# RWKV token shift into a buffer of its own, mixed by GpSimd beside the selective attention

## What is computed

```python
for l in range(DEPTH):                                  # DEPTH = 2
    h = rms_norm_2(x, norm_mix[l])
    cols_a, cols_b, gate_a, gate_b = split_cols(h @ w_in[l], IN_SIZES)   # 1792, 1224, 1024, 1024 columns
    y_a, v_first = rwkv7_branch(cols_a, v_first, rwkv_mu[l], ...)
    y_b = dsa_branch(cols_b, ...)                       # selective attention: 64 keys of 256 for each query
    merged = (sigmoid(gate_a) * (y_a @ w_branch_a[l]) + sigmoid(gate_b) * (y_b @ w_branch_b[l]))
    x = x + merged @ w_out[l]
...
def rwkv7_branch(cols, v_first, mu, ...):
    cols = cols + (token_shift(cols) - cols) * mu       # token_shift: row t gets row t - 1, row 0 gets zeros
    r, k, v, wd, ad, gd = split_cols(cols, RWKV_SIZES)
    w_log = -softplus(-(w0 + tanh(wd) @ w2)) - 0.5
    a = sigmoid(a0 + ad @ a2)
    g = sigmoid(gd) @ g2
...
```

## Time and profile before

| | before |
|---|---|
| median of 3 runs | 3055.31 us |
| lowest and highest | 3055.24 and 3057.67 us |
| the profiled execution | 3050.5 us |
| its span, first to last instruction | 3048.7 us |
| TensorE (matmuls) busy | 2824.4 us, 93% |
| VectorE (DVE) busy | 1524.6 us, 50% |
| ScalarE (ACT) busy | 1037.8 us, 34% |
| GpSimd (POOL) busy | 124.1 us, 4% |
| mean granted TensorE clock | 0.972 |

### The profile page before, as it was taken

The page is one execution under the profiler, slowest core; times in us unless marked ns, Lnnn a source line. Parts: engine busy times, 40 slices in busy tenths (PEclk is TensorE's granted clock), DMA queues, the critical chain, the costliest instruction groups (busy, mean ns, idle before and its releaser), DMA issues.

```text
span 3048.7 us, 34473 instructions
## 1 busy us (share of the span) xinstructions
PE 2824.4 (93%) x14731; PEld 2086.1 (68%) x14731; DVE 1524.6 (50%) x1814; ACT 1037.8 (34%) x1240; POOL 124.1 (4%) x109
## 2 busy tenths in 40 slices
PE   8996999999999999998879999998799889999998
PEld 6774576887878576884437458855374578888887
DVE  3555515445554524443564345435653356666587
ACT  3432223343443223431220133413201245445465
POOL 0002000000011100000002000000020000000000
PEclk9998999999999999998999999999899899999999
DMA  6552144556544153554341435543404056566596
GB/s 251 208 166 83 56 153 151 175 195 200 185 163 155 56 186 121 204 166 138 102 129 33 151 116 202 183 154 98 133 30 154 19 207 227 201 217 228 198 317 240
DMA packets 226724, 484.01 MB, mean 159 GB/s; under 512 B 11694, under 2 KB 45102, under 8 KB 226126
## 3 DMA queue, kind: packets, MB, share of 16 engines
q1 hardware_dynamic: 226192, 478.16, 46.2%
q10 hardware_dynamic: 380, 3.66, 0.4%
HBM read 477.07 MB, written 2.95 MB: 157 GB/s over the span
## 4 chain that ended last, share of the span: by engine, by line
PE 80%; DVE 11%; DMA 3%; ACT 2%; issue 2%; SPq 1%; POOL 0%; ACTq 0%; DVEq 0%; POOLq 0%
PE psum L406 21%; PE psum L403 16%; PE psum L405 16%; PE psum L404 16%; PE psum L1932 2%; PE psum L761 2%; PE psum L524 1%; PE psum L736 1%; PE psum L2662 1%; DMA weight_ring<-in_ffn_w_gate 1%; PE psum L2018 1%; DVE weight_ring_low_halves L398 1%; DVE stage_area_halves L515 1%; ACT weight_high_halves L392 1%; PE psum L746 1%
## 5 line engine op out<-in xcount | busy, mean ns | idle before, releaser
L398 DVE TENSOR_TENSOR weight_ring_low_halves<-weight_ring,weight_high_halves 128x2048 fp32r<-128x2048 f32 (+2 forms) x306 | 656.1, 2156 | 638.0 <-ACT weight_high_halves L392 638.0
L403 PE MATMUL psum<-weight_high_halves,stage_area_halves 128*128 128x512 f32 (+2 forms) x2266 | 875.8, 386 | 56.5 <-DVE stage_area_halves L515 37.7
L405 PE MATMUL psum<-weight_high_halves,stage_area_halves 128*128 128x512 f32 (+2 forms) x2266 | 866.4, 382 | 0.0
L404 PE MATMUL psum<-weight_ring_low_halves,stage_area_halves 128*128 128x512 f32 (+3 forms) x2060 | 788.2, 383 | 0.0
L392 ACT ACTIVATE weight_high_halves<-weight_ring 128x2048 fp32r<-128x2048 f32 (+2 forms) x306 | 551.6, 1812 | 592.5 <-PE psum L405 338.2
L406 PE MATMUL psum<-weight_ring,stage_area 128*128 128x512 f32 (+2 forms) x1600 | 666.4, 577 | 9.2 <-issue 6.6
L406 PEld LDWEIGHTS psum<-weight_ring,stage_area 128*128 128x128 f32 x1600 | 301.5, 191 | 357.5 <-issue 352.4
L403 PEld LDWEIGHTS psum<-weight_high_halves,stage_area_halves 128*128 128x128 f32 x2266 | 431.2, 190 | 146.0 <-issue 25.5
L405 PEld LDWEIGHTS psum<-weight_high_halves,stage_area_halves 128*128 128x128 f32 x2266 | 430.7, 190 | 86.6
L404 PEld LDWEIGHTS psum<-weight_ring_low_halves,stage_area_halves 128*128 128x128 f32 x2060 | 392.0, 190 | 75.5
L505 ACT ACTIVATE stage_area<-psum 128x512 f32<-128x512 f32 (+3 forms) x138 | 76.4, 561 | 702.2 <-PE psum L406 359.9
(11 more groups left out here) (265 smaller groups left out, 2240.4 us busy)
## 6 DMA issues: line engine op xcount, KB each, us to landing
weight_ring<-in_ffn_w_down SPq DMA_DIRECT2D x44, 1024.0 KB, 5.0
weight_ring<-in_ffn_w_gate SPq DMA_DIRECT2D x40, 1024.0 KB, 5.2
weight_ring<-in_ffn_w_up SPq DMA_DIRECT2D x40, 1024.0 KB, 5.1
weight_ring<-in_w_in SPq DMA_DIRECT2D x36, 1024.0 KB, 5.1
weight_ring<-in_moe_wd SPq DMA_DIRECT2D x30, 1024.0 KB, 4.9
weight_ring<-in_moe_wg SPq DMA_DIRECT2D x23, 1024.0 KB, 6.6
weight_ring<-in_moe_wu SPq DMA_DIRECT2D x23, 1024.0 KB, 7.3
weight_ring<-in_mem_w_kv SPq DMA_DIRECT2D x16, 1024.0 KB, 5.1
```

The source lines that it names most:

```text
L398: v.raw.tensor_tensor(self.low_half(name), self.in_slot(name), self.high_half(name), ALU.subtract).then_inc(*v.mark("low_halves", ("halves ...
L403: pe.raw.matmul(out, a[1], w[0], start=start, stop=False)
L404: pe.raw.matmul(out, a[0], w[1], start=False, stop=False)
L405: return pe.raw.matmul(out, a[0], w[0], start=False, stop=stop)
```

## The change

- The shifted rows get a buffer of their own, `shifted_rows`, over the last two slots of `weight_high_halves`, which nothing uses in this stage. VectorE clears row 0 of it ahead of the selective attention's preparation, after a wait for the last four split pieces (L2412 of the new kernel).
- ScalarE issues the three DMAs of the shift right behind the copies of the `a_in` projection, in front of its copies of the turned queries and keys.
- `mix_vector` becomes `mix_gpsimd`: the same three operations, on GpSimd (L1721, L1724, L1726 of the new kernel). VectorE waits for `mixed` after the attention.
- `mu` is no longer a parameter load that waits for the end of the attention. It is a piece of the weight ring, between the pieces of gate block (0, 0) and (0, 1).
- The vectors `vec` wait for the end of the attention, not for `mixed`. Their place in SyncE's queue, behind the pieces of gate block (1, 1), is unchanged.

```diff
@@ Net.__init__
+            self.shifted_rows = names.enter_context(nc.sbuf_tensor("shifted_rows", [P, (HIGH_SLOTS - 2) * SLOT], F32))
+            names.enter_context(nc.sbuf_tensor("up_to_norm_params", [P, 2 * MT * D], F32))
@@ Second.__init__
-        self.colsS = net.part(E, MT, N_A)
-        self.mu = net.part(16896, N_A)
+        self.colsS = net.shifted_rows[:, 0:MT * N_A].rearrange("p (m n) -> p m n", m=MT)
...
+                if (nb, j) == (0, 1):
+                    net.piece(("mu", l), [(slice(0, P), 0, N_A, row_broadcast(ins["rwkv_mu_2"][l], N_A))], 1, SLOT)
                 if (nb, j) == (1, 0):
                     net.piece(("rwkv_small", l), small, 1, SLOT)
-                if (nb, j) == (1, 1):
-                    net.load_param(("mu", l), self.mu, row_broadcast(ins["rwkv_mu_2"][l], N_A), [(f"dsa{l}", "oT", 1)])
...
-                net.load_param(("vec", l, j), self.vec[:, j, :], src, [("mixed", l)], topic="loaded_rwkv_vectors")
+                net.load_param(("vec", l, j), self.vec[:, j, :], src, [(f"dsa{l}", "oT", 1)], topic="loaded_rwkv_vectors")
@@ shift_scalar
-        act.wait_ge(*act.at(*net.proj_names(self.layers[l]["a_in"]), (f"dsa{l}", "oT", 1), ("zero_row", l)))
+        act.wait_ge(*act.at(*net.proj_names(self.layers[l]["a_in"]), ("zero_row", l)))
...
-    def mix_vector(self, v, l):
...
+    def mix_gpsimd(self, pool, l):
+        A, B, mu = self.colsA, self.colsS, self.net.in_slot(("mu", l))[:, 0, 0:N_A]
+        pool.wait_ge(*pool.at(("shift", l, 1)))
+        pool.raw.tensor_tensor(B, B, A, ALU.subtract).then_inc(*pool.step())
+        pool.wait_ge(*pool.last)
+        pool.wait_ge(*pool.at(("loaded", ("mu", l))))
+        pool.raw.tensor_tensor(B, B, widen(mu, 1, MT), ALU.mult).then_inc(*pool.mark("mix_read", ("used", ("mu", l))))
+        pool.wait_ge(*pool.last)
+        pool.raw.tensor_tensor(A, A, B, ALU.add).then_inc(*pool.mark("columns_mixed", ("mixed", l)))
@@ Second.scalar
             net.proj_copy(act, st["a_in"], rot, copy(self.colsA))
+            self.shift_scalar(act, l)
             net.turn_copy(act, self.dsa_turn(l))
             self.index_scalar(act, l)
             self.gate_scalar(act, l, 0, 0)
             attn_scalar(net, act, f"dsa{l}", self.dsa_heads(l))
-            self.shift_scalar(act, l)
@@ Second.vector
+            ahead = net.split_pieces.index("router") if l else net.split_pieces.index(("ffn_dense", "gate", 0, 0))
+            v.wait_ge(*v.at(*[("used", name) for name in net.split_pieces[ahead - HIGH_SLOTS:ahead]]))
+            v.raw.memset(self.colsS[0:1, 0, :], 0.0).then_inc(*v.mark("zero_row_ready", ("zero_row", l)))
             self.dsa_prepare_vector(v, l)
...
             attn_vector(net, v, f"dsa{l}", self.dsa_heads(l), 4)
-
-            v.wait_ge(*v.at((f"dsa{l}", "oT", 1)))
-            v.raw.memset(self.colsS[0:1, 0, :], 0.0).then_inc(*v.mark("zero_row_ready", ("zero_row", l)))
-            self.mix_vector(v, l)
+            v.wait_ge(*v.at(("mixed", l)))
             self.prepare_vector(v, l)
@@ Second.gpsimd
             rstd(("dsai", l), 20, 2)
+            self.mix_gpsimd(pool, l)
             rstd(("kk", l), 0, 16)
```

More of the change, by code:

```diff
@@ L209, in __init__ @@
             self.branch_gates = names.enter_context(nc.sbuf_tensor("branch_gates", [P, 2 * MT * D], F32))
-            names.enter_context(nc.sbuf_tensor("up_to_norm_params", [P, HIGH_SLOTS * SLOT], F32))
+            self.shifted_rows = names.enter_context(nc.sbuf_tensor("shifted_rows", [P, (HIGH_SLOTS - 2) * SLOT], F32))
+            names.enter_context(nc.sbuf_tensor("up_to_norm_params", [P, 2 * MT * D], F32))
             self.norm_r = names.enter_context(nc.sbuf_tensor("norm_params_low_halves", [P, MORE_SLOTS * SLOT], F32R))
@@ L1716, in shift_scalar @@
         act.raw.dma_start(B[0:1, 1, :], A[P - 1:P, 0, :]).then_inc(*act.mark("rows_shifted", ("shift", l, 1), by=16))
-    def mix_vector(self, v, l):
-        A, B = self.colsA, self.colsS
-        v.wait_ge(*v.at(("shift", l, 1), ("loaded", ("mu", l))))
-        v.raw.tensor_tensor(B, B, A, ALU.subtract).then_inc(*v.step())
-        v.wait_ge(*v.last)
-        v.raw.tensor_tensor(B, B, widen(self.mu, 1, MT), ALU.mult).then_inc(*v.step())
-        v.wait_ge(*v.last)
-        v.raw.tensor_tensor(A, A, B, ALU.add).then_inc(*v.mark("columns_mixed", ("mixed", l)))
-        v.wait_ge(*v.last)
+    def mix_gpsimd(self, pool, l):
[7 more added lines that the diff above has]
+        pool.raw.tensor_tensor(A, A, B, ALU.add).then_inc(*pool.mark("columns_mixed", ("mixed", l)))
     def low_rank_turn(self, l):
```

## The result

| | before | after |
|---|---|---|
| median, 20 runs each on the same chips | 3057.9 us | 3065.9 us |
| lowest and highest | 3049.3 and 3063.4 | 3059.4 and 3074.5 |
| the profiled execution, its span | 3050.5, 3048.7 | 3065.2, 3063.4 |
| mean granted TensorE clock | 0.972 | 0.966 |

The ratio is 1.0027, with a 95% interval of 1.0019 to 1.0036: slower by 8 us, 5.8 to 11. The prediction said slower, which holds, but it put the loss at 36.4 us, some four and a half times the 8.0 measured.

A forecast was written before the change was run, and what follows sets the result against it. The chain of waits was taken to run through VectorE's index stage, the attention, then shift, mixing and the vectors' load to L1818. Issue 6.2 plus holds 46.5 less gain 16.3 made +36.4, so 3092 us, range 3061 to 3099.

The forecast's parts named there:

- Part 1, the issue: Ahead of the attention: ScalarE's shift issue delays the copies of turned queries and keys, cost 6.2 us over both layers.
- Part 2, the length of a hold: GpSimd mixing beside VectorE: each operation of 7.75 us holds a VectorE instruction with two SBUF inputs for its whole length.
- The rival of short holds: GpSimd mixing lets VectorE in every 1.4 us: 11 us a layer, +12, 3067 us; chance 0.09.
- The power of the earlier trace: Sign for short holds: a GpSimd power of 3.81 us did not hold VectorE's L1838, which took its usual 1.23.
- Part 2, the number of holds: VectorE's weighings and mask, L1668 and L1672: three holds of 7.75, 23.3 us a layer, 46.5 in both.
- about 2097: Layer 1: the early value taken for the time in us at which the shifted rows land.
- 2095.5: Layer 1: time in us at which the shifted rows are down if the shift takes the 10.35 of before.
- the late bound: Layer 1: the shift can come up to 5.0 us later, at 2100.5, beside weight pieces in flight.
- 2098.7: Layer 1: time in us before which GpSimd must start for three holds among VectorE's weighings and mask.
- Part 3, the gain: Behind the attention: clearing, shift and mixing leave the chain, the vectors are last; gain 16.3 us, between 11.5 and 21.5.
- the middle of 0 to 5.0: Behind the attention: the 1 MB piece in flight just ahead of the vectors delays them by 2.6 us.
- The case that came true: Rival: shift lands behind the mask, two operations run beside the top keys, one hold a layer; +5.4, 3061 us; chance 0.10.

The follow-up runs named there:

- the two profiles: The changed kernel, unchanged, profiled twice: 3065.2 us first and 3063.2 us in the later second profile.
- with the pieces held back: Changed kernel, but SyncE holds the two 1 MB pieces of gate block (0,1) until the shifted rows have landed: 3091.7 us, ratio 1.0106.
- the first profile of before: The kernel before, unchanged, in its first profiled execution: 3050.5 us; its later second profile took 3061.7 us.

## Why the prediction was wrong

- **Part 1, the issue.** 6.2 forecast, 4.0 measured (+2.4 and +1.6). Right in kind. The third issue takes 0.55 and 0.57 us, where it had taken 1.94 and 2.06 before; with the pieces held back it took 1.54 and 1.99 again. Why it is shorter beside the pieces isn't shown.
- **Part 2, the length of a hold.** Right. The operations take 7.75 us and hold VectorE to their end. The rival of short holds fell: wherever L1683, L1673, L807 or L817 met a mixing operation of GpSimd, they got in only when it had ended. The Trainium skill, SBUF — State Buffer, section Who interferes with whom, is borne out at this length by these holds (7.83 us at L1683, 6.4 at L807). Its other sentence, that an instruction with one SBUF input outside the two-port modes does not contend, is borne out by MAX8 and MATCH_REPLACE8 (0.43 and 0.41 us beside GpSimd). The power of the earlier trace rows stays an exception that no run explains: it lasts 3.81 us, and L1838 beside it, which reads two inputs from SBUF, takes its usual 1.23.
- **Part 2, the number of holds. The step that failed** is "I take an early value, about 2097, since the shift goes by ScalarE's own queue and not behind them." The landing was bounded at 5.0 us later than before, and I took 1.5 (2097 less 2095.5). GpSimd's start was 5.0 and 5.9 later, at the late bound in one layer and beyond it in the other. A queue of its own did not spare the shift: weight pieces and shift together kept the transfer engines some nine tenths busy, and 3.9 MB had to pass (2 x 1.05 and the move's 1.8). The bound was also too low: it added the 5.0 us of one piece alone, while the second piece was in flight beside the whole shift. The decision turned on 2098.7, and I chose the side for which only an assumption spoke. So 46.5 us of holds became 18.0 (8.3 and 9.7). With the shift on time there were the three holds a layer, and the kernel was 33.6 us above the one before beside it, where 36.4 had been forecast.
- **Part 3, the gain.** 16.3 forecast, 15.8 and 16.4 measured in the two profiles; the vectors' load is what ends last. Why it ends there was also right (asked for at T + 13.65), and asking for the vectors earlier gave the largest gain of all. For the piece ahead of them I had chosen the middle of 0 to 5.0, 2.6; in layer 1 it measured 2.5 (11.7 us from the first issue to L1818, instead of 9.2), which is a choice that came out well.
- **Left out.** Behind L1818 nothing was costed. Behind its wait for the vectors, 9.0 us in layer 0 and 6.2 in layer 1, TensorE runs at a granted clock of 0.50, and the stage takes 1.6 us more in layer 1 and 0.9 to 4.9 in layer 0. In the kernel before, the clock is at 0.50 earlier (1560 to 1566 us), in the low-rank products (6.11 us against 3.91), behind the 12.0 us for which TensorE waits for the mixing and ScalarE's step behind it.
- **Sum.** The case that came true had a chance of 0.10 in the text, at +5.4; measured +8.0. That the two lie so near is partly luck: the issue cost 2.2 us less than forecast, the holds 2.5 more (L1681 waits for the second operation too), and the clock's 2.5 to 6.5 us were in no term.

## What to carry to other kernels

An element-wise stream on GpSimd is not free time beside VectorE: count, at the time at which it really runs, the VectorE instructions that read two SBUF operands or are plain SBUF scalings, however small, and charge up to one whole GpSimd instruction for each meeting. (GpSimd's power of the earlier trace rows held nothing, so look for such a meeting in a trace first.) That time hangs on a transfer, so work out its landing with all that is in flight beside it, by bytes and not by queue, and price the forecast on both sides of it. Before work is moved to another engine, look at what ends the stage: here it was a load late in a queue. Asking for it earlier took 17.7 us off the changed kernel (ratio 1.0027 to 0.9969), more than the change had cost. It was not tried on the kernel before, where the vectors lie over the shifted rows and have to wait for the mixing.

## What the runs showed of the hardware

- A tensor_scalar of 128 x 2 in SBUF waited 6.4 us for the end of a GpSimd operation of 7.73 us, and one of 512 columns waited in the same way (7.83). TENSOR_REDUCE from SBUF (0.69 us) and SCALAR_TENSOR_TENSOR with one operand in PSUM (0.68) ran beside it unchanged.
- GpSimd's long operations hardly change their length whether VectorE waits for them or not: 7.72 to 7.81 us, and 8.02 once, where it started in the middle of VectorE's weighings.
- A load of 1 MB and a move of 1.6 MB inside SBUF, issued within 0.6 us of each other on two queues and behind another load, took 16.7 us instead of 5.0 and 13.9 instead of 8.0. The load that was issued 2.3 us ahead of the move kept its 5.0.
- The same attention took 26.4, 28.8 or 30.8 us, in versions of the kernel whose mixing did not run beside it. In the one of 26.4 (the first profile of before) the granted clock is 0.50 from 1510 to 1516 us and 0.66 in the next 6; in that of 28.8 (the second) it is 0.51, 0.50 and 0.56 in the three stretches of 6 us from 1514 on. Single profiles of this kernel can't be compared to better than some 5 us here.
